# Combining expert outputs: old rows, norm and next parameters loaded into freed weight slots; y of every tile summed on TensorE; stores of layer 0 awaited later

## What is computed

```python
h = _layer_norm(ALPHA * h + mix, *norms[i][0]).astype(dt)
h = _layer_norm(ALPHA * h + _hier_moe(h, *moes[i]), *norms[i][1]).astype(dt)
...
hid = jax.nn.silu(xblk @ w_gate[e]) * (xblk @ w_up[e])
return hid @ w_down[e]
...
y = jnp.zeros((T + 1, d), F32).at[slot_tok].add(yb.astype(F32) * slot_gate[:, None])
```

## Time and profile before

| | |
|---|---|
| median of 3 runs | 2360.32 us (2356.91 to 2366.04) |
| profiled execution, its own time | 2361.56 us |
| its span, first to last instruction | 2359.4 us |
| TensorE busy | 2193.0 us, 93% |
| VectorE, ScalarE, GpSimd busy | 33%, 21%, 13% |
| combining of layer 0 | last scatter issued at 1179.06, next stage's first product at 1250.08 |
| combining of layer 1 | last scatter issued at 2300.59, end 2359.4 |
| moved by DMA | 529.81 MB, mean 225 GB/s |

### The profile page before, as it was taken

How to read it: one execution, slowest core, us unless ns; L and a number is a source line. 1 busy time by engine, 2 the same in 40 slices (tenths; PEclk the granted TensorE clock), 3 DMA queues, 4 the chain that set the end, 5 groups by cost and what they waited for, 6 DMA issues and landing times. The chain is left out here.

```text
span 2359.4 us, 33583 instructions
## 1 busy us (share of the span) xinstructions
PE 2193.0 (93%) x13491; PEld 1245.3 (53%) x13491; DVE 767.2 (33%) x1608; ACT 486.2 (21%) x904; POOL 309.0 (13%) x263
## 2 busy tenths in 40 slices
PE   8999999999689999999968999999968999999994
PEld 5778656655454455455434555555545455545541
DVE  7652236643611111111173344443251111111116
ACT  2222246611010001000033544431101000000001
POOL 7252000011011111111030000001101111111102
PEclk9999999999789999999988999999968999999998
DMA  4110001112399999899884111111139999989987
GB/s 159 38 37 1 21 1 72 32 46 71 152 393 419 420 419 418 332 407 409 357 299 163 40 40 27 33 39 46 62 152 380 413 419 419 419 348 391 414 368 306
DMA packets 148199, 529.81 MB, mean 225 GB/s; under 512 B 43874, under 2 KB 66946, under 8 KB 131664
## 3 DMA queue, kind: packets, MB, share of 16 engines
q1 hardware_dynamic: 134608, 493.84, 53.2%
q0 software_dynamic: 13312, 33.84, 3.8%
q10 hardware_dynamic: 128, 0.02, 0.0%
HBM read 499.99 MB, written 39.98 MB: 229 GB/s over the span
## 5 line engine op out<-in xcount | busy, mean ns | idle before, releaser
L1857 PE MATMUL l_main_pgu<-l_w_ring,l_ex_xT 128*64 128x256 f32 (+1 forms) x4992 | 474.1, 385 | 12.7 <-DMA l_w_ring<-in_l_moe_w_gate 9.8
L1857 PEld LDWEIGHTS l_main_pgu<-l_w_ring,l_ex_xT 128*64 128x64 f32 (+1 forms) x4992 | 285.6, 129 | 190.4 <-issue 40.9
L1903 PE MATMUL l_main_py<-l_w_ring,l_ex_hT 128*64 128x512 f32 (+1 forms) x1248 | 231.9, 594 | 1.9 <-DVE l_ex_hT L1974 1.9
L1854 PE MATMUL l_main_pgu<-l_w_ring,l_ex_xT 128*128 128x512 f32 x384 | 170.1, 596 | 3.3 <-DMA l_w_ring<-in_l_moe_w_gate 3.3
L1970 DVE TENSOR_TENSOR l_ex_hid<-l_ex_sil,l_main_pgu 128x256 f32<-128x256 f32 (+1 forms) x76 | 35.2, 464 | 377.0 <-PE l_main_pgu L1857 279.8
L1974 DVE COPY l_ex_hT<-l_main_ph 128x256 f32<-128x256 f32 (+1 forms) x76 | 35.5, 467 | 365.9 <-PE l_main_ph L1878 365.9
L2315 PE MATMUL lru_pr<-h2T,lru_wz 128*128 128x352 f32 (+1 forms) x480 | 144.4, 461 | 10.3 <-ACTq L2370 10.3
L2333 PE MATMUL lru_pg<-h2T,lru_wz 128*128 128x512 f32 x320 | 148.7, 592 | 0.0
L1903 PEld LDWEIGHTS l_main_py<-l_w_ring,l_ex_hT 128*64 128x64 f32 (+1 forms) x1248 | 69.1, 127 | 132.1 <-issue 124.8
L1946 ACT ACTIVATE l_ex_sil<-l_main_pgu 128x256 f32<-128x256 f32 (+1 forms) x76 | 31.8, 418 | 468.9 <-PE l_main_pgu L1857 374.7
L2315 PEld LDWEIGHTS lru_pr<-h2T,lru_wz 128*128 128x128 f32 x480 | 92.6, 193 | 63.1 <-ACTq L2370 10.7
(11 more groups left out here) (465 smaller groups left out, 2728.0 us busy)
## 6 DMA issues: line engine op xcount, KB each, us to landing
l_w_ring<-in_l_moe_w_gate SPq DMA_DIRECT2D x64, 2048.0 KB, 27.0
l_w_ring<-in_l_moe_w_up SPq DMA_DIRECT2D x64, 2048.0 KB, 27.9
l_w_ring<-in_l_moe_w_down SPq DMA_DIRECT2D x64, 2048.0 KB, 33.4
l_y<-expert_rows SPq DMA_DIRECT2D x32, 512.0 KB, 8.2
h_rows<-H SPq DMA_DIRECT2D x24, 512.0 KB, 5.3
lru_wz<-in_l_w_in SPq DMA_DIRECT2D x20, 512.0 KB, 4.9
w_in<-in_l_w_in SPq DMA_DIRECT2D x4, 2048.0 KB, 8.9
H<-h_rows SPq DMA_DIRECT2D x16, 512.0 KB, 9.9
```

The source lines that it names most:

```text
L1854: last = pe.matmul(out[:], x[:, k, :], w[0][:, k, :], start=k == 0, stop=k == KD - 1)
L1857: last = pe.matmul(out[HALF * h + o:HALF * h + o + m, 0:256], x[:, k, it.at + o:it.at + o + m], w[n][:, k, 256 * h:256 * h + 256], start=k ...
L1903: last = pe.matmul(py[b][HALF * h + o:HALF * h + o + m, :], hT[:, c % 2, HALF * (c // 2) + o:HALF * (c // 2) + o + m], ws[n][:, c, 512 * h ...
```

## The change

- SP's program in the experts gets `unit_used(unit)`. After the last weight load it waits until the last units in slots 6, 7 and 8 are used, and loads all h1 rows of the combining into that space (`load_rows`: 9 loads in layer 0, 8 in layer 1). Then it waits for slot 9, and loads gain and bias of the norm there, and in layer 0 the eight parameter loads of the recurrent stage (`load_norm`).
- The combining loads only the two y rows of a tile, 6 tiles ahead instead of 4, and frees a buffer when the sum is made, not when VectorE has used it.
- TensorE sums y of tile 0 too; VectorE's two passes over it go, and its sum reads the h1 row from `rows` and writes `H`.
- In layer 0 the two weight loads of the recurrent stage go out ahead of store 3; the wait for the stores moves to the recurrent stage, ahead of the residual loads of its output projection.
- Small tiles of the recurrent stage are placed elsewhere, so that its parameters don't overlap the new buffers.

```diff
@@ experts_and_combine, SP
+            for unit in range(3 * NE):
+                if unit + UNITS >= 3 * NE and unit % UNITS in ROW_UNITS:
+                    unit_used(unit)
+            combine.load_rows(sp)
+            for unit in range(3 * NE):
+                if unit + UNITS >= 3 * NE and unit % UNITS == NORM_UNIT:
+                    unit_used(unit)
+            combine.load_norm(sp)
             sp.wait_ge(ya_ready, acts[N])
             sp.wait_ge(yv_ready, dves[N])
             over.sync(sp)
@@ class Combining
-    BUFFERS = 4
+    BUFFERS = 6
...
+    def load_rows(self, sp):
+        for i in range(self.first, NT):
+            t0, m = TILES[i]
+            sp.dma_start(self.rows[0:m, i, :], self.K.h1_dram[t0:t0 + m, :]).then_inc(self.h1_loaded, 16)
+
+    def load_norm(self, sp):
+        self.norm.load(sp, self.A[self.L + "_ln2_g"], self.A[self.L + "_ln2_b"])
+        if not self.last_layer:
+            self.K.lru.load_parameters(sp)
@@ sync
             if j >= B:
-                sp.wait_ge(self.z_done, 2 * (j - B + 1))
+                sp.wait_ge(self.y_summed, 2 * (j - B + 1))
             for k in range(2):
                 sp.dma_start(self.y[k][j % B][0:m, :], K.y_dram[k * T + t0:k * T + t0 + m, :]).then_inc(self.loaded[j % B], 16)
-            sp.dma_start(K.H[0:m, self.first + j, :], K.h1_dram[t0:t0 + m, :]).then_inc(self.loaded[j % B], 16)
...
-            if j == 1:
-                norm.load(sp, self.A[self.L + "_ln2_g"], self.A[self.L + "_ln2_b"])
         for j in range(self.n):
             if j + B < self.n:
                 load(j + B)
+            if j == self.n - B and not self.last_layer:
+                K.lru.load_weights(sp, 0, 0)
+                K.lru.load_weights(sp, 1, 1)
             store(j)
-            if j == self.n - B - 1 and not self.last_layer:
-                K.lru.load_weights(sp, 0, 0)
-                K.lru.load_parameters(sp)
-                K.lru.load_weights(sp, 1, 1)
-        sp.wait_ge(self.stored, 16 * self.n)
+        if self.last_layer:
+            sp.wait_ge(self.stored, 16 * self.n)
@@ vector
+        dve.wait_ge(self.h1_loaded, 16 * n)
-            if j == 0:
-                dve.wait_ge(self.loaded[0], 48)
-                do(dve.scalar_tensor_tensor(out=z, in0=z, scalar=ALPHA, in1=self.y[0][0][0:m, :], op0=ALU.mult, op1=ALU.add))
-                dve.tensor_tensor(z, z, self.y[1][0][0:m, :], ALU.add).then_inc(self.z_done, 2)
-            for h in range(2 if j else 0):
+            for h in range(2):
...
@@ rglru_and_project, SP
             sp.wait_ge(gate_ready, NG * NB)
+            sp.wait_ge(*K.h2_stored)
             project.sync(sp)
```

More of the change, by code:

```diff
@@ L1749, in _, with unit_used @@
         def _(sp):
+            def unit_used(unit):
+                r, kind = W.units[unit]
+                i = W.last[r]
+                if kind == GATE:
+                    sp.wait_ge(g_ready, i + 1)
+                elif kind == UP:
+                    sp.wait_ge(u_ready, i + 1)
+                elif by_dve[i]:
+                    sp.wait_ge(yv_ready, dves[i + 1])
+                else:
+                    sp.wait_ge(ya_ready, acts[i + 1])
             for u in range(HEAD_UNITS, 3 * NE):
@@ L1755, in _ @@
                 if u >= UNITS:
[L1756 to L1765, removed]
-                load_unit(sp, E, u, kind, e, E.loaded[u % UNITS])
+                    unit_used(u - UNITS)
+                load_unit(sp, E, u, kind, e, E.loaded[u % UNITS])
+            for unit in range(3 * NE):
[6 more added lines that the diff above has]
+            combine.load_norm(sp)
             sp.wait_ge(ya_ready, acts[N])
@@ L2131, in __init__ @@
         self.y = [[at(f"{L}_y{k}{i}", [D]) for i in range(self.BUFFERS)] for k in range(2)]
+        assert self.last_layer or at.at <= K.lru.loaded_at
+        unit_at = lambda unit: (K.base + 31) // 32 * 32 + unit * KD * F * 4
+        at = Place(nc, unit_at(NORM_UNIT) - NT * D * 4)
+        assert at.at >= unit_at(ROW_UNITS[0]) and (self.last_layer or at.at >= K.lru.loaded_end)
+        self.rows = at(f"{L}_h1_rows", [NT, D])
         self.norm = Norm(nc, K, L + "_ln2", at, self.first)
-        assert self.last_layer or at.at <= K.lru.wz_at
+        assert at.at <= unit_at(NORM_UNIT + 1)
         sem = lambda n: K.sem(f"{L}_cb_{n}")
@@ L2136, in __init__ @@
         self.loaded = [sem(f"loaded{i}") for i in range(self.BUFFERS)]
-        self.y_summed, self.z_done, self.order, self.turned, self.hT_ready, self.stored = map(sem, (
-            "y_summed", "z_done", "order", "turned", "hT_ready", "stored"))
+        self.y_summed, self.z_done, self.order, self.turned, self.hT_ready, self.h1_loaded = map(sem, (
+            "y_summed", "z_done", "order", "turned", "hT_ready", "h1_loaded"))
+        self.stored = nc.alloc_semaphore(f"{L}_cb_stored")
         self.ps, self.pt = ps, pt
+        if not self.last_layer:
+            K.h2_stored = self.stored, 16 * self.n
+    def load_rows(self, sp):
[4 more added lines that the diff above has]
+        self.norm.load(sp, self.A[self.L + "_ln2_g"], self.A[self.L + "_ln2_b"])
+        if not self.last_layer:
+            self.K.lru.load_parameters(sp)
     def sync(self, sp):
@@ L2178, in vector @@
             m = TILES[i][1]
[L2179 to L2184 removed]
+            for h in range(2):
                 c = slice(512 * h, 512 * h + 512)
[L2186 to L2187 removed]
+                dve.wait_ge(self.y_summed, 2 * j + h + 1)
+                dve.scalar_tensor_tensor(out=K.H[0:m, i, c], in0=self.rows[0:m, i, c], scalar=ALPHA, in1=self.ps[j % 2][h][0:m, :],
+                                         op0=ALU.mult, op1=ALU.add).then_inc(self.z_done, 1)
             dve.wait_ge(self.z_done, 2 * j + 2)
@@ L2200, in y_sum @@
             m = TILES[first + j][1]
-            pe.wait_ge(self.loaded[j % B], 48 * (j // B + 1))
+            pe.wait_ge(self.loaded[j % B], 32 * (j // B + 1))
             if j >= 2:
@@ L2249, in __init__ @@
         assert K.route_constants.free <= at.at and K.route_constants.start >= self.wz_at + 2 * 2 * P * 4
-        self.prm, self.pc = at("lru_prm", [9, NB]), at("lru_pc", [9])
-        self.m = [at(f"lru_m{i}", [NB]) for i in range(4)]
+        self.prm = at("lru_prm", [9, NB])
+        self.loaded_end = at.at
         self.gg, self.ra, self.ii, self.a, self.t = (at("lru_" + n, [T]) for n in ("gg", "r", "i", "a", "t"))
+        self.pc, self.m = at("lru_pc", [9]), [at(f"lru_m{i}", [NB]) for i in range(4)]
         assert at.at <= K.w_out1_at
```

4 lines of the change are left out of this document (3 added, 1 removed).

## The result

The changed kernel takes 2367.52 us (median of 16 runs, 2363.74 to 2372.55). The kernel before, on the same chips, takes 2361.20 us (16 runs, 2354.53 to 2369.59). The ratio is 1.0025, with a 95% interval of 1.0016 to 1.0034. By the medians that is 6.3 us slower, by the ratio 5.9 (3.8 to 8.0): small, but clear of the noise, and outside the forecast range of 2349 to 2365.

What follows compares the result with a forecast made beforehand. TensorE was busy 93% of the span, leaving only seams at the two combining stages. Terms -7.4 (layer 0 tail) + 3.4 (layer 0 start) + 1.1 (layer 1 start) = -2.9 us, from 2360.32 to 2357.4 us; range 2349 to 2365.

Steps and rivals of the forecast that it cites:

- The tail of layer 0: End of layer 0's combining: without the store wait and late stores, TensorE starts the next stage at 1242.7, gaining 7.4 us.
- The steady part: Combining from tile 2 on: VectorE sets the pace at 4.83 us a tile, so the change gains nothing there.
- Layer 1: Start of layer 1's combining: the last scatter meets the tail of the rows, T0 = 2312.8, loss 1.1 us.
- Layer 0: Start of layer 0's combining: moved loads fill the DMA queue ahead of y, T0 = 1191.1, loss 3.4 us.
- 1.0 us of SP time each: Layer 0's eight parameter loads ahead of y: SP needs 8 us for them and is free at 1181.5.
- 1.5 us a load: Sign for layer 0: the forecast is wrong if SP's parameter issues take over 1.5 us each.
- the queue's bytes: DMA queue ahead of y in layer 0: 24.3 us of work from 1166, so it reaches y at 1190.3.
- SP blocked at the element-wise loads ahead of y: Rival, layer 0: eight parameter issues at 3.35 us each, loss 14.9, sum +8.6 us, 2368.9 us; chance 0.15.
- T0 = 1194: Layer 0: the T0 from which the blocked-SP rival decides, as a loss of 6.3 with layer 1's 1.1 eats the 7.4.
- T0: Start of a combining stage: the time at which y of tile 0 has landed; break-even 1187.7 in layer 0, 2311.7 in layer 1.
- the chain from T0 to tile 2: Start of a stage: TensorE sums tile 0, then tile 1; tile 2 starts 14.8 us after T0 in layer 0, 14.3 in layer 1.
- Full gain: Rival, both layers: scatters pass the rows and small loads cost the queue nothing, -10.4 us, 2349.9 us; chance 0.28.

Runs made afterwards that it cites:

- e2: The kernel before, with only the wait for layer 0's h2 stores moved to the recurrent stage, ahead of the residual loads: 2355.78 us, ratio 0.9965.
- e3: e1 with tile 0 summed on VectorE in two passes again: 2356.97 us, ratio 0.9972 to the kernel before.
- e4: e3 with only the h1 rows of tiles 0 and 1 loaded early, the others with their y: 2348.14 us, ratio 0.9951 to the kernel before.
- e1: The changed kernel with the eight parameter loads moved behind the recurrent weight loads: 2360.52 us, ratio 0.9994 to the kernel before.
- e5: e4 with the eight parameter loads ahead of y again, as in the changed kernel: 2353.29 us, ratio 0.9961 to the kernel before.
- e6: e1 plus 13 unused products per layer between last expert and first sum, to raise TensorE's clock: 2370.66 us, ratio 1.0034 to the kernel before.
- e7: e4 plus 14 unused products per layer between last expert and first sum, to raise TensorE's clock: 2358.74 us, ratio 0.9982 to the kernel before.
- e10: The same edit as e4, timed again: 2348.86 us, ratio 0.9943 to the kernel before.

## Why the prediction was wrong, point by point

**The tail of layer 0: right.** Forecast a gain of 7.4 us, measured 7.5. The view of SP's waits has no wait for the h2 stores at the stage's end any more, and e2 shows 5.3 of it from the moved wait alone, where the 5.2 of the earlier trace rows were to go. What came next was ScalarE's last copy, as the prediction had it.

**The steady part: right.** 4.83 us a tile before and after. Early rows and six y buffers give nothing there.

**Layer 1: right in mechanism, and in the sum with some luck.** Forecast +1.1, measured +1.3. Three of its terms were off and nearly cancel: y's first load went out 6.9 us after the last scatter, not 5.9; it took 4.9 us to TensorE's first sum, not 6.3; and from there to tile 2 it took 14.9, not 14.3. The last scatter no longer met idle engines: it landed after 6.3 us. By e3 and e4 this is 3.1 us at the first y load (7.04 against 3.93), and the sum of tile 0 on TensorE another 1.6 at tile 2 (e1 against e3); what both took from the start, the early rows gave back in part. The Trainium skill, DMA: Bandwidth & Descriptors, "Queues, rings and completion order", lets each DMA engine take packets of its queues in turn. From that the prediction worked out a scatter that the rows hardly delay. The traces disagree with that estimate: 3.3 to 3.7 us with two rows loaded early, 6.3 to 7.1 with all. Whether the scatter loses this time by the order of the packets or in another way they do not show.

**Layer 0: wrong, +10.4 instead of +3.4.** The step that failed is "SP has 1172.5 + 1.0 + 8 = 1181.5 for its own issues, which alone would fit", that is, "1.0 us of SP time each". That 1.0 came from the earlier trace rows, where the DMA engines had little left to do (53 GB/s in 1230 to 1232). Here they went in behind nine rows and the norm, and the eight took 19.91 us, not 8; SP was free at 1195.87, not at 1181.5. That is over the 1.5 us a load that the prediction had named as a sign of being wrong. The forecast counted the queue's bytes (until 1190.3) and SP's issues as two separate things and took the later. But SP was held at one issue for 11.49 us, from 1176.43 on, while the queue drained, and at the next for 3.01; the y loads, behind them on SP, could not even be issued meanwhile. Only then did the rest go out at the price of the forecast. The bytes were undercounted too: the bias, the last of the large loads, landed at 1175.48 + 15.6 = 1191.1, some 1188 on the clock of before, where the sum without the parameters has 1190.3 - 5.6 = 1184.7. The mechanism is that of the rival "SP blocked at the element-wise loads ahead of y", but not in the form in which it was priced, 3.35 us at each of the eight: the time was lost at two. The 3.35 was no single dear issue in the kernel before either; the weight load ahead of it had taken 3.18 (line 2262, at 1221.59). The point that this rival gave, T0 = 1194, was passed by far: on its scale TensorE's first sum stands at 1179.06 + 18.01 = 1197.1. e1 takes these loads away and gets 6.7 us back; e5 keeps them and takes the rows away, and SP needs 10.75 us for the eight.

Of the 10.4 us, e1 gives 6.7 to the parameters. e3 gives 2.7 to tile 0's place on TensorE. The rest, 24.37 - 23.43 = 0.9 us, stands in e3: there the scatter under the rows costs 3.3 us at tile 2 (24.37 against the 21.09 of e4), and e4 in turn is 2.3 under before, with norm and two rows in place before y.

**The clock: a smaller error in the same sum.** The prediction took the chain from T0 to tile 2 from tile 1 of before, 14.8 and 14.3 us. It took 15.8 and 14.9. The window at 1200.06 shows what was missed: tile 0 of layer 0 has 16 rows, and over the 8.94 us in which TensorE is busy with these sums and the first of tile 1 the granted clock reads 0.50 (1.2 GHz). In layer 1 the products have 128 rows; the window from 2317.41 reads 0.50 too, but the next one, from 2322, reads 0.88, the mean of a stretch in which it rises to 2.4 GHz. e6 confirms that this is the clock and not the sums: with it raised beforehand, the same chain is 4.0 and 2.4 us shorter than in e1.

**Full gain, at 0.28, was given too much.** It needed the scatter to pass the rows, which e4 against e3 refutes, and y summed on TensorE from T0 = 1186.0, that is 6.9 us after the last scatter. In e6, with all rows queued, TensorE isn't there before 9.85 us; in e7, with two, it is at 6.97. So with the change's own loads that case could not have come out whole in such an execution, and what sets the time at which TensorE is free for y was not tried.

**The range** ended at 2365 because the blocked SP was left out with 0.15. The bounds of its own terms would have told otherwise: a single moved issue had no measured price behind a full queue, only one at 1.0 and one at 3.35, and these ends lie 8 times 2.35 = 18.8 us apart on SP. The measured 19.91 us for eight lie between them.

**What stays open.** Which limit holds SP at an issue (bytes, pieces or loads outstanding) was not tried. Why TensorE is free for y between 7.1 and 11.6 us after its last expert product is open as well. The profiled execution of e7 was the fastest of its ten runs, 2349.86 us against a median of 2358.74: its two combining stages take 6.0 and 4.3 us more than those of e4, but its last scatter of layer 0 came 6.2 us earlier (1174.22), for no reason of the edit. e4 and e10, the same code, differ by 1.5 us at tile 2 of layer 0 (21.09 and 22.59), so differences of a microsecond between single executions are not read as effects here.

## What to carry to other kernels

A load that is moved under other work is hidden from the compute engines, but not from the engine that issues it nor from the event behind it: ask which loads stand ahead of it in the queue, what the same engine has to issue next, and whether the scatter or store that releases that next load has to share the DMA engines with it. Load early only what the first tiles need. A price of an issue read where the queue was empty does not hold where it is full. And try the cheap part of a change alone: one moved wait (e2) gained 8.3 us by the ratio, where the whole change lost 5.9.

## What the runs showed of the hardware

Four element-wise loads of 5 KB held SP for 4.1 us with little queued, for 5.6 us behind two rows and the norm (e5) and for 15.7 us behind nine rows and the norm (changed kernel). Of the 15.7 us one issue took 11.49, while the DMA engines moved 348 to 412 GB/s, and less only towards its end (255 in 1186 to 1188).

The last scatter lands in 3.2 and 3.8 us with nothing loaded early (e2), in 3.1 to 4.0 with two rows and the norm (e4, e10), in 4.9 with the parameters behind them (e5, layer 0) and in 6.3 to 7.2 with nine or eight rows (changed kernel, e1, e3). Single executions stray: 5.4 in layer 1 of e7 with two rows, 8.5 in layer 1 of e6 with eight.

Through 8.94 us of TensorE busy with mostly 16-row products the granted clock read 0.50. Where 128-row products came first (e6), the same 16-row products ran at 1.00, and in 1208 to 1210, with tile 1's 128-row products behind them and no gap, the clock read 0.50 again.

From TensorE's last expert product to the first product that waits for no data it takes 11.61 and 9.78 us in e6, 8.72 and 7.14 in e7; no wait of the trace shows this time as long as the next operand is later than that.
